# A one-layer encoder trunk: the front of the later tiles in named pieces with a slot table per engine, 23 rows of tile 0 and none of tile 1 added on VectorE, past keys loaded in whole rows

## What is computed

```python
xn = rmsnorm(x, norm1)
z  = xn @ w_in                     # (1024 -> 3400), split into the groups A and B
# A: gated linear recurrence, 4 heads of 128 x 128 state
f = lb + (1 - lb) * sigmoid(af);  S = diag(f) S + (1 - f) i^T;  o = S^T silu(aq)
a_out = rmsnorm_head(o) * silu(ag)
# B: index scores choose the top keys of each query, attention over those keys alone
score = sum_h iw_h * relu(iq_h . ik);  keep = top_k(score);  b_out = softmax(q . k[keep]) @ v[keep]
h = x + concat(a_out, b_out) @ w_o
# PEER: 16384 experts of one neuron, 8 heads, 16 experts per head and token
q = rmsnorm(h) @ wq;   s1, s2 = q_half1 @ subkeys1, q_half2 @ subkeys2
eidx, g = top16 of the sums of top16(s1) and top16(s2), softmax of their scores
y = h + sum over 8 * 16 experts of g * gelu(rmsnorm(h) . u[eidx]) * v[eidx]
```

## Time and profile before

| | us |
|---|---|
| median of 3 runs (lowest, highest) | 1228.69 (1225.39, 1234.05) |
| the profiled execution, device time | 1229.14 |
| its span | 1227.3 |

### The profile page before, as it was taken

The page is one execution under the profiler, slowest core; times in us unless marked ns, Lnnn a source line. Parts: engine busy times, 40 slices in busy tenths (PEclk is TensorE's granted clock), DMA queues, the critical chain, the costliest instruction groups (busy, mean ns, idle before and its releaser), DMA issues. The chain is left out here.

```text
span 1227.3 us, 11548 instructions
## 1 busy us (share of the span) xinstructions
PE 1051.3 (86%) x3275; PEld 522.6 (43%) x3275; DVE 807.0 (66%) x1961; ACT 504.8 (41%) x1477; POOL 455.8 (37%) x445
## 2 busy tenths in 40 slices
PE   9997998889789897878888997989986887787786
PEld 5766444544456434534433553446432322232222
DVE  2637666668858566366897765666786677766755
ACT  2636233544544333336536433344432333333332
POOL 0004353433333242343434542343543544354431
PEclk9998999879999998898979999999999999999999
DMA  9958999988798999697999999999999999999997
GB/s 377 402 208 318 348 423 422 354 356 329 300 407 309 391 389 413 260 358 290 423 414 372 388 421 421 418 420 414 388 426 420 421 422 422 421 422 421 422 421 306
DMA packets 70336, 468.12 MB, mean 381 GB/s; under 512 B 7928, under 2 KB 11008, under 8 KB 18944
## 3 DMA queue, kind: packets, MB, share of 16 engines
q0 software_dynamic: 55296, 402.68, 81.0%
q1 hardware_dynamic: 14976, 64.70, 13.2%
HBM read 462.86 MB, written 4.42 MB: 381 GB/s over the span
## 5 line engine op out<-in xcount | busy, mean ns | idle before, releaser
L1958 PE MATMUL PSUM<-UV,DIAG 128*128 128x512 f32 x1272 | 630.6, 628 | 107.4 <-ACT DIAG L993 106.4
L1468 DVE CUSTOM_DVE_ANT_0 UV<-UV,PSUM 128x1024 f32<-128x1024 f32 x336 | 404.5, 1219 | 210.8 <-DMA UV<-in_p_uv,EIDX 207.2
L566 POOL DMA_INDIRECT UV<-in_p_uv,EIDX x336 | 325.0, 967 | 530.0 <-PE PSUM L1958 485.0
L1958 PEld LDWEIGHTS PSUM<-UV,DIAG 128*128 128x128 f32 x1272 | 234.7, 197 | 433.0 <-ACT DIAG L993 224.8
L982 ACT ACTIVATE GELU<-DOTS 128x1 f32<-128x1 f32 x384 | 77.2, 201 | 445.8 <-DVE DOTS L1468 443.0
L993 ACT ACTIVATE DIAG<-CST,WGT 128x128 f32<-128x128 f32 x366 | 147.0, 402 | 12.0
L1958 PE MATMUL PSUM<-EIGHTH,DIAG 128*128 128x512 f32 x192 | 100.5, 649 | 41.5 <-ACT DIAG L993 41.3
L566 POOL DMA_INDIRECT EIGHTH<-in_p_uv,EIDX x48 | 46.2, 962 | 217.2 <-PE PSUM L1958 116.2
L985 ACT ACTIVATE WGT<-GELU,GATE 128x1 f32<-128x1 f32 x384 | 113.2, 295 | 15.3 <-DVE GATE L1304 2.9
L1958 PEld LDWEIGHTS PSUM<-EIGHTH,DIAG 128*128 128x128 f32 x192 | 35.5, 199 | 92.5 <-ACT DIAG L993 55.1
L1468 DVE CUSTOM_DVE_ANT_0 EIGHTH<-EIGHTH,PSUM 128x1024 f32<-128x1024 f32 x48 | 58.2, 1213 | 23.3 <-DMA EIGHTH<-in_p_uv,EIDX 22.9
(11 more groups left out here) (296 smaller groups left out, 935.0 us busy)
## 6 DMA issues: line engine op xcount, KB each, us to landing
WR<-in_w_o SPq DMA_DIRECT2D x13, 512.0 KB, 11.5
UV<-in_p_uv,EIDX POOLq DMA_INDIRECT x336, 11.4
WR<-in_p_wq SPq DMA_DIRECT2D x10, 512.0 KB, 14.8
UV<-in_w_o SPq DMA_DIRECT2D x2, 2048.0 KB, 14.7
UV<-in_p_wq SPq DMA_DIRECT2D x2, 2048.0 KB, 9.8
WR<-in_w_B SPq DMA_DIRECT2D x2, 2048.0 KB, 7.9
UV<-in_w_B SPq DMA_DIRECT2D x4, 512.0 KB, 6.5
UV<-in_w_B SPq DMA_DIRECT2D x2, 1024.0 KB, 11.2
```

The source lines that it names most:

```text
L566: nc.gpsimd.indirect_dma_start(ROWS[place_of(n)], None, a["p_uv"], bass.IndirectOffsetOnAxis(EIDX[:, n:n + 1], 0)).then_inc(row_got[place_ ...
L1468: v.tensor_tensor_reduce(out=row, in0=row, in1=XNP, scale=1.0, scalar=0.0, op0=ALU.mult, op1=ALU.add, accum_out=DOTS[:, n % NW:n % NW + 1] ...
L1958: ins = mm(bank[6 + k][:, :], DIAG[:, m % ND, :], VROW[place_of(n)][:, k * 512:(k + 1) * 512], start=n == 0, stop=ends)
```

## The change

The numbers are replaced by names. Each generator yields a name, and a table per engine (`PE_AT`, `ACT_AT`, `DVE_AT`, `POOL_AT`) holds the slot of every name. Pieces are cut smaller on DVE (five steps of a list of the top 16, the four scans of the logs, the index scores head by head), on ACT (dot products, keys and queries apart) and on PE (dot products one by one, keys and queries apart). What is computed in a piece, the order of the pieces within `trunk()` and the PSUM places stay as they were, but for the copies of unit AG 0 and of `pv` on ACT, which change places. SP's order is unchanged.

`ADDED` has 23 rows of tile 0 at uneven distances; tile 1 has none, as before. The sum of tile 1 now starts with row 128 itself, and `X[1]` is added at n = 255. The arrays of the past keys get 16 zero columns behind every 256, so that one transfer fills whole rows of 8.5 KB; ACT then writes the new keys over the zeros, as before.

```diff
-UNIT_SLOT = [1, 7, 13, 19, 25, 30, 35, 42, 50, 56, 64, 70, 78, 84]
...
-def in_slots(front):
-
-    due = next(front)
+def in_slots(front, at):
+
+    def follow():
+        x = next(front, ALL + 1)
+        return at[x] if isinstance(x, str) else x
+
+    due = follow()
...
-ADDED = [*range(5, 96, 6), 382, 383]
+PE_AT = {
...
+    "AF 0.0": 32, "AF 0.1": 34, "AF 0.2": 36, "AF 0.3": 38, "keys 1": 38, "queries 1": 38, "AF 1.0": 40, "AF 1.1": 41,
+    "AF 1.2": 43, "AF 1.3": 44, "dots 1.00": 45, "dots 1.01": 45, "dots 1.10": 45, "dots 1.11": 45, "AI 1.0": 49,
...
+ADDED = [
+    5, 8, 10, 17, 24, 32, 34, 41, 46, 47, 50, 66, 68, 71, 73, 79, 83, 86, 88, 92, 101, 116, 120, 382, 383
+]
 SUMMED = [n for n in range(HEADS * PK) if n not in ADDED]
+FIRST_SUMMED = [min(n for n in SUMMED if n >= t * SLOTS) for t in (0, 1)]
...
-            sp.dma_start(KTS[:, :, 0:PAST], a["kt"].rearrange("p (b s) -> p b s", b=BD_)).then_inc(kts_in, 16)
+            sp.dma_start(KTS.rearrange("p b s -> p (b s)"), a["kt"]).then_inc(kts_in, 16)
...
-                yield 49
                 for par in range(2):
-                    out_dots(1, par)
+                    for g in range(2):
+                        yield f"dots 1.{par}{g}"
+                        out_dots(1, par, g)
+                yield "log 1"
                 log_f(1)
...
-                if n < SLOTS and n - 1 in ADDED:
-                    add(n - 1, X[0], X[0], row_added)
+                if n - 1 in ADDED and n < 383:
+                    add(n - 1, X[(n - 1) // SLOTS], X[(n - 1) // SLOTS], row_added)
...
-                    add_h(t, True)
+                    if t == 2:
+                        add_h(t, True)
...
-                    ends = n == 2 * SLOTS - 1 or n == SUMMED[-1]
+                    starts, ends = n in FIRST_SUMMED, n == SUMMED[-1]
...
-                if n == SLOTS - 1:
-
-                    pe.wait_ge(row_added, done_before(SLOTS, ADDED))
-                    add_h(0, False)
+                if n in (SLOTS - 1, 2 * SLOTS - 1):
+
+                    pe.wait_ge(row_added, done_before(n + 1, ADDED))
+                    add_h(t, False)
```

More of the change, by code:

```diff
@@ L124, with whole @@
 PLACE = places()
+def whole(pieces):
+    for _ in pieces:
+        pass
 class Turns:
@@ L976, in _ @@
             out_xt(1)
-            first(-1)
+            first(1)
             def weigh(n):
@@ L1244, in choose @@
                 if (t, h) == (0, 0):
-                    yield from top16(own, v, lists, slot, 5, range(2))
+                    yield from top16(own, v, lists, name + " lists", range(2))
                     own.caught_up()
@@ L1252, in choose @@
                     own.done(v.max_index(FI[:, 0:8].bitcast(U32), FV[:, 0:8], few))
-                    yield from decode(t, h, 0, 8, slot + 1, 3)
-                    yield from top16(own, v, lists, slot, 5, range(2, 5))
-                else:
-                    yield from top16(own, v, lists, slot, 5)
-                yield slot + 1
+                    yield from decode(t, h, 0, 8, name + " few", 3)
+                    yield from top16(own, v, lists, name + " lists", range(2, 5))
+                else:
+                    yield from top16(own, v, lists, name + " lists")
+                yield name + " pairs"
                 own.caught_up()
@@ L1266, in choose, with decode @@
                 else:
[L1267 to L1268 removed]
+                    yield from top16(own, v, [(row, FV, FI.bitcast(U32))], name + " pairs")
+                yield name + " decode"
                 own.caught_up()
[L1270 to L1272 removed]
+                yield from decode(t, h, 8 if (t, h) == (0, 0) else 0, PK, name + " decode")
+            def decode(t, h, lo, hi, name, bits=4):
                 k, n, j = slice(lo, hi), hi - lo, slice(0, 1 << bits)
@@ L1282, in decode @@
                 if n == PK:
-                    yield slot + 1
+                    yield name + " places"
                 own.done(v.tensor_tensor(OH[:, :, k, j], OH[:, :, k, j], wide(SIF[:, :, j], 2, n), ALU.mult))
+                if n == PK:
+                    yield name + " sum"
                 own.done(v.tensor_reduce(EPART[:, :, k], OH[:, :, k, j], axis=AX, op=ALU.add))
@@ L1366, in trunk @@
                 own.done(v.memset(SCORE[:, KS:KS + SPARE], DUMMY), wz_ready)
-                yield 144
-                sums_of_logs(2)
-                yield 150
+                yield "bounds 2"
+                yield from sums_of_logs(2)
+                yield "scores 2"
                 pb = take(dve, ("sc",))
@@ L1425, in _ @@
             penalty(0, SCORE[:, 0:P])
-            keys(0)
+            whole(keys(0))
             maxima(0, 0, 0)
-            queries(0)
+            whole(queries(0))
             maxima(0, 1, 0)
@@ L1562, in unit @@
                 name = unit_name(chunk, k)
-                for part, slot in enumerate((0, 1, 3, 4)):
-                    yield UNIT_SLOT[n] + slot
+                for part in range(4):
+                    yield f"{chunk} {k}.{part}"
                     w = later_weights(chunk)
```

469 lines of the change are left out of this document (298 added, 171 removed), and 53 rows, old and new, of tables (ACT_AT, DVE_AT, PE_AT, POOL_AT).

## The result

The changed kernel takes 1171.01 us (median of 4 runs, 1168.92 to 1175.78) against 1227.88 us for the kernel before in the same session: a ratio of 0.9535 with a 95% interval of [0.9488, 0.9583]. The forecast was 1188 us in a range of 1163 to 1222. The profiled execution took 1172.46 us with a span of 1170.6 us. So 56.9 us went where 41 were expected.

What follows compares the result with a forecast made beforehand. No engine was full; gathers at 421 GB/s were the floor, with 84.3 us lost to engines waiting on each other. Gains 33.0 + 7 + 2 + 1 = 43.0, less 2, took 1229.1 to 1188 us, range 1163 to 1222.

Steps and rivals of the forecast that it cites:

- rival B: Whole kernel: the tables fit nearly everywhere, losses fall to the start and some 15 us more; 1168 us, chance 0.14.
- Waits beside tile 0's rows: VectorE's waits for other engines in tile 0's rows shrink by 52.4 us through more slots of room; gain 33.0 us.
- factor of 0.63: Beside tile 0's rows: lost transfer per us of VectorE's wait, 54.5 us against 87.1; the 8 buffers absorb the rest.
- Tile 1's rows: Of 22.0 us of transfer lost beside tile 1's rows, a third comes back: gain 7 us, between nothing and 15.
- Tile 2's rows: Some choices stand a few slots later, but the gathers are the bound there: 0 us, a loss only in the rivals.
- rival D: Slower: TensorE waits for banks in some eight places, and late choices cost in tile 2; 1248 us, chance 0.07.
- Seven rows more on VectorE: Tile 0's rows: 12.0 us of work leave TensorE, VectorE gets 9.0; gain 2 us, between -3 and +6.
- Past keys in whole rows: Past key loads: whole rows in place of 1 KB pieces gain 1 us beyond the query's wait, between -0.3 and +4.
- End of tile 1: `X[1]` goes in behind row 255, adding 1.72 us there and saving as much at row 128: 0, between -2 and +2.
- The 2 us for unnamed waits: Whole kernel: 2 us taken off the summed gain for new waits that could not be named.
- Rival A: Whole kernel: the engines' load is the bound, not the order, so waits go but work stays; 1209 us, chance 0.22.
- Rival C: Whole kernel: waits come back one slot on, gains and new waits cancel; 1225 us, chance 0.09.

Runs made afterwards that it cites:

- slots_old: The changed kernel with all four tables at the old slots, except ScalarE's copies of AF 0 and AG 0, two and one slots later: 1202.16 us, ratio 0.9799.
- one_wait: The changed kernel with tile 1's index dots back at slot 48 on TensorE and its sums of logs at 51 on VectorE: 1173.25 us, ratio 0.9557.
- added_even: The changed kernel with the 16 evenly spaced added rows of the kernel before: 1182.52 us, ratio 0.9627.
- rows_alone: The kernel before with only the past keys loaded in whole rows: 1216.23 us, ratio 0.9894.
- rows_undone: The changed kernel with the past keys loaded in 1 KB pieces again: 1184.18 us, ratio 0.9643.
- keys_behind: The kernel before, still with 1 KB pieces, both past key loads moved behind tile 1's last query weights in SyncE's order: 1215.84 us, ratio 0.9866.

## Why the prediction was right, and where it was off

The direction, the range and the place were right. The size was not quite: 1171.0 lies just below the forecast's own span (1172 to 1204) and nearest to rival B (1168), whose account of the transfer that stays lost, 23 us, fits the measured 25.8 better. By the steps of the sum:

- **Waits beside tile 0's rows, 33.0 us.** Right in kind and size. 5 of them (8 x 0.63) were the query weights and belong to the whole rows. The rest, 28, compares with row 128 in slots_old and after: 512.6 - 486.6 = 26.0 us. That came of two small errors against each other: 47 us of waiting went where 44 (52.4 without the gate's 8) were forecast, and the factor of 0.63 measured as 0.55. Entry by entry I gave too little: the forecast was some 41 us of waiting left, 25.2 were. The logs kept 0.8 instead of 3.2, the output projection nothing instead of 5.7, the key products 0.2 instead of 4.7. For the logs one_wait shows why: they had inherited lateness that went with the units ahead of them; for the other two the same is likely and not shown. The added rows kept all of their 9.7, where I had expected 3.6, and the first choice of tile 1 got shorter (4.6 to 3.3) instead of longer.
- **Tile 1's rows, 7 us.** Right: rows 128 to 255 take 358.7 us in slots_old and 352.4 after, 6.3 us.
- **Tile 2's rows, 0.** Off by 3.6 us in the profiled executions (322.2 in slots_old against 325.8), the loss that I had put into rival D.
- **Seven rows more on VectorE, +2 between -3 and +6.** This step failed: the rows are worth 11.5 us with the new tables (added_even) and up to 14.1 with the old ones (slots_old against rows_alone, which differ in more than the rows). "With the gathers as the bound the 12 us are no gain by themselves" holds for the count: 23 even rows give nothing, and 15 more in tile 1 nothing. But I priced only the count and took the uneven distances for a detail. With the new tables the gathers are not the bound in rows 60 to 79, TensorE is, and there the change puts five of its rows (66, 68, 71, 73, 79) and keeps TensorE from reaching the penalty early and falling to the lower clock. With the old tables the same rows do nothing in that stretch (75.2 us in slots_old, 76.0 in rows_alone); what the up to 14.1 us come from there is open.
- **Past keys in whole rows, +1 beside the 5 in the waits.** The cause was right (the weights queued behind the keys, TensorE's wait, the gate), the size was half: 11.7 us alone and 13.2 us within the change. I multiplied VectorE's 8.4 us of wait by 0.63 as if the buffers could absorb it. In the kernel before they didn't, because the buffers themselves were held: TensorE's wait kept them full and GpSimd stood 13.77 us ahead of gather 121 (4.04 in rows_alone). So the whole 8.4 us went and 6.6 us of other waits behind it with them, 15.0 us in rows 120 to 127. In rows_undone they absorbed a part: 18.4 us of TensorE's waits there cost 13.2. The landing of `in_kt` in under 15 us came in rows_alone (14.1) and not in the changed kernel (16.2). The Trainium skill ("DMA: Bandwidth & Descriptors", Specifications) puts the minimum for line rate at 512 B, by which 1 KB pieces cost nothing. For the engines as a whole the traces agree: with these pieces under way they moved 414 GB/s before (442 to 472 us) and 412 in rows_undone and keys_behind. What the rule does not tell is when the load itself lands beside the gathers: 29.5 to 31.9 us against 14.1 to 16.2 for whole rows.
- **End of tile 1, 0**, wasn't tested by itself. **The 2 us for unnamed waits** weren't needed.

Read from the runs, 56.9 us are 31.2 for the tables, 11 to 14 for the added rows with what comes along, 12 to 13 for the whole rows. That 31.2, 14.1 and 11.7 add up to the whole says nothing by itself, as these three runs are one chain from before to after; that the other two, undone from the changed kernel, gave 11.5 and 13.2 says that the parts depend little on each other. The forecast had some 35, 2 and 6 for them: the total fell inside the range since the tables were priced well, and two smaller terms were too small. *Rival A* (load) was wrong for the kernel as a whole, whose windows beside tile 0's rows show 397 to 417 GB/s, and right for rows 60 to 79. *Rival C* is out. Of *rival D* the bank waits are small, 2.9 us in slot 40 to 42, and those of tile 2 are real. How far TensorE lagged in each of the eight places I have not read.

## What to carry to other kernels

Look at what stands behind a slow transfer in its queue before asking what the transfer costs: moving two loads that nobody needed yet gave 14.6 us, making them twice as fast 11.7. Taking work off an engine pays where that engine is busy without a break, and not just ahead of a place where it waits for another; so look at windows of 20 rows for the place, as the average share of a kernel doesn't show it. A wait of TensorE can cost more than its length, when the clock granted behind it is the lower one. A wait that a stretch of program inherits from lateness ahead of it goes when that lateness goes, so not each wait needs its own room. But a wait of the engine that frees the buffers is not simply absorbed by them: 10.3 us of it cost 11.7 before, and 18.4 us cost 13.2 in the changed kernel.
